# FFN stages of a two-model kernel: third block's split ahead of the norm's variance, squares inside the second block, row sums a block later

## The chip, the cores and the metric

One core of one Trainium2 chip. The metric is the device time of one execution in microseconds; three runs of the kernel before were timed, and one more execution was profiled. TensorE multiplies matrices into PSUM, ScalarE (ACT) and VectorE (DVE) do the elementwise work, GpSimd (POOL) helps with both, SyncE (SP) issues the large transfers.

## The reference

Two stacks of two layers each, over one sequence of 256 tokens of width 1024 (fp32). The first stack modulates each stage by vectors computed from a condition `c`; the second has plain RMS norms:

```python
# first stack, for l in 0, 1
mod = silu(c) @ mod_w[l] + mod_b[l]              # nine vectors of 1024: shift, scale, gate of three stages
f = swiglu(modulate(x, sh1, sc1), ffn_in[l, 0], ffn_out[l, 0])
x = deepnorm_residual(x, f, g1, ln_g[l, 0], ln_b[l, 0], 0.5)
...                                              # a mixer (even or odd), then a second FFN in the same form
# second stack, for i in 0, 1
h = x + 0.5 * swiglu_2(rms_norm_2(x, norm_ffn1[i]), w_ffn1_in[i], w_ffn1_out[i])
...                                              # window attention and a convolution
h = h + 0.5 * swiglu_2(rms_norm_2(h, norm_ffn2[i]), w_ffn2_in[i], w_ffn2_out[i])
x = h + (p[i] @ w_pe_proj[i]) * sigmoid(rms_norm_2(h, norm_pe[i]) @ w_pe_gate[i])

def swiglu_2(x, w_in, w_out):
    gate, up = split(x @ w_in, 2)
    return (silu(gate) * up) @ w_out
def rms_norm_2(x, g, eps=1e-6):
    return x * rsqrt(mean(x * x) + eps) * g
```

The inner width of an FFN is 2816.

## The kernel before

**Stream of weights.** All weights pass as a stream of 1 MB blocks (128 x 2048 fp32) through a ring of four slots `raw`. SyncE issues the transfer of block n when block n-4 is done (`blk_done`). A matmul in fp32 is made of three in a rounded format, so each block is split: ScalarE writes the high part, `whi` (`split_hi`, line 471), VectorE the rest, `wlo` (`split_lo`, line 1039), and TensorE waits for it (`split_ready`). Both splits run `AHEAD` = 2 blocks ahead of the block in hand. Each engine has its own program, and its instructions run in the order written; a helper `catch_up` makes the split of the second block of a stage inside the norm ahead of it.

**An FFN.** 22 blocks go up (a gate block and a value block form a pair, 11 pairs), 11 go down. In the first stack `ffn_pair` is the elementwise work of a pair, in the second `ffn2_pair`. The up stage runs as a loop of five turns of two pairs, and the last pair stands behind the loop.

**Second stack.** The activations go into TensorE before they are divided by the norm's root, and the factor is applied to the result. `wide_block` (lines 1879 and 1881) writes high and low parts side by side into one of two banks pairs, `ab` and `mb`. `ffn2_pair` on ScalarE copies the low half out (655), splits the next block, applies Silu (658), copies the second low half (660), splits, and rounds the product (664). On VectorE it adds the low half to the bank (1095), multiplies by `rstd` (1097, which also frees the bank), splits, adds for the second bank (1101), multiplies with GpSimd's part (1105, which frees the second bank), splits, and writes `h_lo`. GpSimd multiplies the gate by `rstd` (445).

**The norm ahead of it** (`norm2`, with `which` 0 and 2 ahead of FFNs): VectorE updates x, ScalarE writes `u_hi` and squares (632), VectorE writes `u_lo` (1323) and sums the squares (1329); TensorE sums them over partitions (`squares`, 2123) behind the first block; ScalarE takes the Sqrt (649) and VectorE the reciprocal (1362), at the end of `norm2`. The split of the third block comes behind all this, inside the first pair.

**First stack, down stage.** `d_block` (1987) does a down block. The vectors of the modulation are summed over partitions on the side: VectorE multiplies slices of `mod_w` by `c` and adds them (1127, 1130), ScalarE makes the high part of such a vector (`vec_high`, 522; for v >= 2 it waits for the sums of vector v-2), GpSimd the low part (`vec_low`, 414), TensorE sums them (`mod_rows`, 2045 and 2046; it waits for the take of the vector before), and VectorE takes the result (`mod_take`: 1143 for a gate, 1148 and 1152 for the others). The first and third FFN have six vectors, five of them in this stage, the second has three and the fourth one. With many vectors VectorE also has one product step 1130 behind each split.

## Time and profile before

| | us |
|---|---|
| median of 3 runs (2372.4 to 2381.05) | 2380.95 |
| the profiled execution | 2381.47 |
| its span, from first to last instruction | 2379.7 |
| TensorE matmuls busy | 2258.0 |
| VectorE busy | 1733.5 |
| ScalarE busy | 1232.8 |
| GpSimd busy | 219.3 |

The profile's page lists busy times, and the trace behind it each instruction. A row of a timeline has start, duration, engine, line, operation, written and read tiles, and in brackets how long the engine had been idle before it and what ended that. The mean granted clock of TensorE was 0.986 of its full level.

### The profile page before, as it was taken

What the parts mean: (1) busy time and instruction counts of PE and PEld (TensorE: products, weight loads), DVE (VectorE), ACT (ScalarE), POOL (GpSimd) and SP (SyncE); (2) the same over time, 40 slices, a digit from 0 to 9 for tenths busy, and PEclk for the clock granted to TensorE, in tenths of its full rate; (3) what the DMA queues carried; (4) which work ended last, traced back from release to release, by engine and by line L of the source; (5) the groups of instructions that cost most, each with busy time, mean ns of one, the idle gap of its engine ahead of it and who ended that gap; (6) DMA issues with size and microseconds to landing.
All of it is one profiled execution on the core that took longest, in us unless ns stands there. A gap on an engine that the chain in (4) does not pass through costs nothing.

```text
span 2379.7 us, 38110 instructions
## 1 busy us (share of the span) xinstructions
PE 2258.0 (95%) x15380; PEld 2072.6 (87%) x15380; DVE 1733.5 (73%) x1813; ACT 1232.8 (52%) x1301; POOL 219.3 (9%) x199
## 2 busy tenths in 40 slices
PE   4999889999999998999999999999999999999999
PEld 4997788799889877799788997988998899798899
DVE  5997786796589976755677569977567756996665
ACT  2443555454454545455466454666456636466644
POOL 0123000010201300000021000011001100001200
PEclk9999999999999999899999999999999999999999
DMA  8996432586568752455455542445454554345453
GB/s 345 350 357 230 153 142 108 214 312 259 194 236 355 299 209 91 160 212 179 175 190 189 186 154 104 158 179 188 183 182 159 189 182 160 107 153 179 181 188 135
DMA packets 75934, 471.49 MB, mean 198 GB/s; under 512 B 8707, under 2 KB 8963, under 8 KB 27580
## 3 DMA queue, kind: packets, MB, share of 16 engines
q1 hardware_dynamic: 53136, 383.80, 43.7%
q0 software_dynamic: 18976, 68.71, 7.7%
q10 hardware_dynamic: 3724, 17.56, 2.0%
q8 instruction: 75, 1.23, 0.2%
q14 instruction: 23, 0.19, 0.0%
HBM read 468.97 MB, written 1.06 MB: 198 GB/s over the span
## 4 chain that ended last, share of the span: by engine, by line
PE 77%; DVE 12%; ACT 6%; DMA 3%; issue 2%; ACTq 0%; SPq 0%; DVEq 0%
PE ab L1848 30%; PE acc L1848 13%; PE acc L1987 9%; PE ab L1879 7%; PE mb L1879 6%; DVE wlo L1039 3%; PE ab L1881 3%; PE mb L1881 3%; ACT whi L471 2%; DMA raw<-stream 2%; PE mb L2234 1%; DMA par<-params 1%; DVE sc L1659 1%; PE acc L2262 1%; DVE sc L1130 1%
## 5 line engine op out<-in xcount | busy, mean ns | idle before, releaser
L1039 DVE TENSOR_TENSOR wlo<-raw,whi 128x2048 fp32r<-128x2048 f32 x361 | 827.3, 2295 | 317.2 <-ACT whi L471 315.2
L471 ACT ACTIVATE whi<-raw 128x2048 fp32r<-128x2048 f32 x361 | 689.4, 1912 | 472.9 <-DMA raw<-stream 297.7
L1848 PE MATMUL ab<-uu,whi 128*128 128x256 f32 x4512 | 830.4, 287 | 25.2 <-DVE uu L1227 11.7
L1848 PEld LDWEIGHTS ab<-uu,whi 128*128 128x128 f32 x4512 | 711.6, 194 | 40.1 <-issue 22.8
L1848 PE MATMUL ab<-uu,wlo 128*128 128x256 f32 x2256 | 643.2, 285 | 0.0
L1848 PEld LDWEIGHTS ab<-uu,wlo 128*128 128x128 f32 x2256 | 437.7, 194 | 0.0
L1848 PE MATMUL acc<-h_hi,whi 128*128 128x256 f32 (+1 forms) x1032 | 293.8, 285 | 4.3 <-ACT sc L853 1.6
L1848 PE MATMUL acc<-h_hi,wlo 128*128 128x256 f32 (+1 forms) x1032 | 292.4, 283 | 0.0
L1848 PE MATMUL acc<-h_lo,whi 128*128 128x256 f32 (+1 forms) x1032 | 292.4, 283 | 0.0
L1879 PE MATMUL ab<-uu,whi 128*128 128x512 f32 x704 | 252.0, 400 | 8.7 <-DVE uu L1323 4.9
L1879 PE MATMUL mb<-uu,whi 128*128 128x512 f32 x704 | 249.9, 398 | 0.0
L1848 PEld LDWEIGHTS acc<-h_hi,whi 128*128 128x128 f32 x1032 | 197.7, 192 | 6.1 <-DVE h_lo L1743 2.0
L1881 PE MATMUL ab<-uu,wlo 128*128 128x256 f32 x704 | 198.4, 282 | 0.0
L1848 PEld LDWEIGHTS acc<-h_lo,whi 128*128 128x128 f32 x1032 | 197.7, 192 | 0.1
L1848 PEld LDWEIGHTS acc<-h_hi,wlo 128*128 128x128 f32 x1032 | 197.7, 192 | 0.0
L1881 PE MATMUL mb<-uu,wlo 128*128 128x256 f32 x704 | 197.4, 280 | 0.0
L445 POOL TENSOR_TENSOR sc<-sc,rstd 128x512 f32<-128x512 f32 x44 | 98.2, 2231 | 991.4 <-ACT sc L658 991.4
L1879 PEld LDWEIGHTS ab<-uu,whi 128*128 128x128 f32 x704 | 133.6, 190 | 42.6 <-issue 9.5
L1879 PEld LDWEIGHTS mb<-uu,whi 128*128 128x128 f32 x704 | 132.6, 188 | 31.4
L1130 DVE SCALAR_TENSOR_TENSOR sc<-modmem,cact,sc 128x1024 f32 (+1 forms) x112 | 152.3, 1360 | 8.2 <-DVE h_lo L1086 2.7
L1987 PE MATMUL acc<-whi,h_hi 128*128 128x512 f32 x448 | 148.7, 396 | 2.5 <-DVE wlo L1039 2.5
L1987 PE MATMUL acc<-wlo,h_hi 128*128 128x512 f32 x448 | 147.6, 394 | 0.0
(338 smaller groups left out, 2734.7 us busy)
## 6 DMA issues: line engine op xcount, KB each, us to landing
raw<-stream SPq DMA_DIRECT2D x365, 1024.0 KB, 4.8
modmem<-mods POOLq DMA_DIRECT2D x128, 512.0 KB, 6.1
sc<-lnrows ACTq DMA_DIRECT2D x5, 1024.0 KB, 5.2
sc<-start ACTq DMA_DIRECT2D x4, 1024.0 KB, 16.7
gateb<-gaterows ACTq DMA_DIRECT2D x6, 512.0 KB, 3.7
hank<-toep POOLq DMA_DIRECT2D x8, 192.0 KB, 3.8
x<-xT ACTq DMA_DIRECT2D x1, 1024.0 KB, 31.5
x<-xn ACTq DMA_DIRECT2D x1, 1024.0 KB, 4.8
```

What stands on the lines that cost most here:

```text
L445: nc.gpsimd.tensor_tensor(gated, gated, r, ALU.mult).then_inc(g2_ready, 1)
L471: nc.scalar.activation(whi[:, n % RAW, :], raw[:, n % RAW, :], ACT.Copy).then_inc(hi_ready, 1)
L1039: nc.vector.tensor_tensor(wlo[:, n % RAW, :], raw[:, n % RAW, :], whi[:, n % RAW, :].bitcast(F32), ALU.subtract).then_inc(lo_ready, 1)
L1130: nc.vector.scalar_tensor_tensor(out=out, in0=part, scalar=cact[:, k:k + 1], in1=out, op0=ALU.mult, op1=ALU.add).then_inc(mod_done, 1)
L1659: ins = nc.vector.scalar_tensor_tensor(out=sc[:, 28 + c, :], in0=cpad[:, c, t:t + T], scalar=w, in1=sc[:, 28 + c, :], op0=ALU.mult, op1=AL ...
L1848: ins = nc.tensor.matmul(out, l, r, start=first and i == 0, stop=last and i == 2, skip_group_check=True)
L1879: nc.tensor.matmul(bank[:, m, :].rearrange("p (a t) -> p a t", a=2), wh[:, k, m * P:m * P + P], uu[:, :, k, :], start=k == 0, stop=k == DM ...
L1881: ins = nc.tensor.matmul(bank[:, m, 0:T], wl[:, k, m * P:m * P + P], u_hi[:, k, :], start=False, stop=k == DM - 1, skip_group_check=True)
L1987: ins = nc.tensor.matmul(acc[:, 2 * t + c, :], l, w[:, k, 512 * c:512 * c + 512], start=first and k == 0 and w is wh and l is hh, stop=las ...
L2234: ins = nc.tensor.matmul(mb[:, k % 2, o:o + w], l, r, start=(c == 0), stop=(c == len(terms) - 1), skip_group_check=True)
L2262: ins = nc.tensor.matmul(out, v(h, kt), turned(k)[:, kt * T:kt * T + T], start=(kt == 0), stop=(kt == 1))
```

## The change

- `norm2` with `which` 0 or 2: ScalarE splits the third block (`split_hi(g[0] + AHEAD)`) behind the squares and ahead of the wait for the variance; VectorE makes its part behind the sums of squares. The wait for the root and the reciprocal leave `norm2` for these two norms.
- `ffn2`: the first pair is written out ahead of the loop (the last one joins the loop). It has no split in its first half, and VectorE does the reciprocal in it, behind the first add.
- `ffn2_pair`: the add frees the bank, and a separate count `sum_made` tells ScalarE of the products.
- Layer 1's first FFN of the second stack (`ffn2(late=True)`): TensorE does the squares inside the second wide block, half way.
- First stack: `mod_rows(f, v)` stands ahead of block v+3 and no longer v+2, with the take on VectorE ahead of the split of j = v+3 and no longer behind that of j = v+2; `mod_save` and `mod_cols` move from j = 7 to 8.
- `ffn` is written for the first stack alone. That changes no order.

```diff
 # ScalarE
@@ norm2
                 cnt["x"] += 4
                 cnt["var"] += 1
+                if which % 2 == 0:
+                    split_hi(g[0] + AHEAD)
                 act.wait_ge(var_ready, cnt["var"])
@@ ffn2_pair
-            def ffn2_pair(n, k, j, it):
+            def ffn2_pair(n, k, j, it, first=False):
                 b = a[0] + 2 * k
                 done(n + 2 * k, it)
                 nc.scalar.activation(spare_lo[:, 0], part_lo(b), ACT.Copy).then_inc(ylo_ready, 1)
-                split_hi(n + 2 * k + AHEAD, it)
-                act.wait_ge(bank_evac[b % 2], at(b // 2 + 1, it, 2))
+                if not first:
+                    split_hi(n + 2 * k + AHEAD, it)
+                act.wait_ge(sum_made, at(2 * cnt["made"] + 2 * k + 1, it, 4))
                 nc.scalar.activation(gated, gated, ACT.Silu).then_inc(silu_ready, 1)
                 done(n + 2 * k + 1, it)
                 nc.scalar.activation(spare_lo[:, 1], part_lo(b + 1), ACT.Copy).then_inc(ylo_ready, 1)
                 split_hi(n + 2 * k + 1 + AHEAD, it)
-                act.wait_ge(bank_evac[(b + 1) % 2], at((b + 1) // 2 + 1, it, 2))
+                act.wait_ge(sum_made, at(2 * cnt["made"] + 2 * k + 2, it, 4))
@@ ffn2
+            def ffn2(beside=None):
+                ffn2_pair(g[0], 0, 0, None, True)
...
+                with act.Fori(0, 5) as it:
+                    for j in range(2):
+                        ffn2_pair(g[0], j, j + 1, it)
...
 # VectorE
@@ ffn2_pair
-                nc.vector.tensor_tensor(gated, part_hi(b), spare_lo[:, 0], ALU.add).then_inc(sum_made, 1)
-                dve.wait_ge(sum_made, at(2 * cnt["g2"] + 2 * k + 1, it, 4))
+                nc.vector.tensor_tensor(gated, part_hi(b), spare_lo[:, 0], ALU.add).then_inc(bank_evac[b % 2], 1)
+                dve.wait_ge(bank_evac[b % 2], at(b // 2 + 1, it, 2))
+                if first:
+                    dve.wait_ge(std_ready, cnt["std"])
+                    nc.vector.reciprocal(rstd[:, 0, :], rstd[:, 0, :]).then_inc(rinv_ready, 1)
+                    dve.wait_ge(rinv_ready, rinv)
                 nc.vector.tensor_tensor(gated, gated, rstd[:, 0, :].unsqueeze(1).broadcast_to([P, 2, T]),
-                                        ALU.mult).then_inc(bank_evac[b % 2], 1)
-                split_lo(n + 2 * k + AHEAD, it)
+                                        ALU.mult).then_inc(sum_made, 1)
+                if not first:
+                    split_lo(n + 2 * k + AHEAD, it)
...
-                    .then_inc(sum_made, 1)
-                dve.wait_ge(sum_made, at(2 * cnt["g2"] + 2 * k + 2, it, 4))
+                    .then_inc(bank_evac[(b + 1) % 2], 1)
+                dve.wait_ge(bank_evac[(b + 1) % 2], at((b + 1) // 2 + 1, it, 2))
                 dve.wait_ge(g2_ready, at(cnt["g2"] + k + 1, it, 2))
-                nc.vector.tensor_tensor(prod, gated, spare_lo[:, 1], ALU.mult)\
-                    .then_inc(bank_evac[(b + 1) % 2], 1)
+                nc.vector.tensor_tensor(prod, gated, spare_lo[:, 1], ALU.mult).then_inc(sum_made, 1)
@@ ffn (first stack), down stage
                 for j in range(FFN_B - 1):
+                    if 3 <= j <= min(vecs, 5) + 2:
+                        mod_take(f, j - 3)
                     split_lo(g[0] + j + AHEAD)
                     if vecs > 5 and j < DM:
                         mod_block(f, 5 * DM + j, None, j)
-                    if 2 <= j <= min(vecs, 5) + 1:
-                        mod_take(f, j - 2)
-                    if j == 7:
+                    if j == 8:
                         mod_save(f, 1)
                         mod_cols(GATE_AT[f])
@@ norm2
                 sum_squares(3)
+                if which % 2 == 0:
+                    split_lo(g[0] + AHEAD)
                 cnt["sq"] += 4
                 cnt["std"] += 1
-                dve.wait_ge(std_ready, cnt["std"])
-                nc.vector.reciprocal(rstd[:, 0, :], rstd[:, 0, :]).then_inc(rinv_ready, 1)
-                dve.wait_ge(rinv_ready, 4 * l + which + 1)
+                if which % 2:
+                    dve.wait_ge(std_ready, cnt["std"])
+                    nc.vector.reciprocal(rstd[:, 0, :], rstd[:, 0, :]).then_inc(rinv_ready, 1)
+                    dve.wait_ge(rinv_ready, 4 * l + which + 1)
 # TensorE
@@ wide_block
+                    if between is not None and (k, m) == (0, 1):
+                        between(acc[:, 3, 0:T])
@@ ffn (first stack)
                 for i in range(FFN_B - 2):
-                    if 2 <= i <= min(vecs, 5) + 1:
-                        mod_rows(f, i - 2)
+                    if 3 <= i <= min(vecs, 5) + 2:
+                        mod_rows(f, i - 3)
@@ ffn2
-            def ffn2():
+            def ffn2(late=False):
                 wide_block(g[0], a[0], None, True)
                 cnt["u"] += 4
-                squares(acc[:, 3, 0:T])
-                wide_block(g[0] + 1, a[0] + 1)
+                if not late:
+                    squares(acc[:, 3, 0:T])
+                wide_block(g[0] + 1, a[0] + 1, None, False, squares if late else None)
```

## Rows read from the trace of the kernel before

**Rows 1.** The page, busy time: us (share of the span) xinstructions.

```profile
PE 2258.0 (95%) x15380; PEld 2072.6 (87%) x15380; DVE 1733.5 (73%) x1813; ACT 1232.8 (52%) x1301; POOL 219.3 (9%) x199
```

**Rows 2.** Timeline of TensorE, first FFN's down stage.

```profile
183.54 0.39 PE L2045 MATMUL mb<-uu,mean_r 128*128 128x512 f32 x1
...
193.81 0.47 PE L2045 MATMUL mb<-uu,mean_r 128*128 128x512 f32 x1 [3.75 <-issue]
...
201.88 0.40 PE L2045 MATMUL mb<-uu,mean_r 128*128 128x512 f32 x1
```

**Rows 3.** Timeline of VectorE, same stage.

```profile
189.19 3.38 DVE L1130 SCALAR_TENSOR_TENSOR sc<-modmem,cact,sc 128x1024 f32<-128x1024 f32 x1
192.50 1.21 DVE L1143 SCALAR_TENSOR_TENSOR gateb<-mb,gateb 128x1024 f32<-128x1024 f32 x1
```

**Rows 4.** Timeline of TensorE, third FFN's down stage.

```profile
824.42 0.77 PE L2045 MATMUL mb<-uu,mean_r 128*128 128x512 f32 x1 [5.05 <-issue]
...
833.46 0.39 PE L2045 MATMUL mb<-uu,mean_r 128*128 128x512 f32 x1
```

**Rows 5.** Timeline of TensorE, last pair of both down stages.

```profile
232.99 0.47 PE L1987 MATMUL acc<-whi,h_hi 128*128 128x512 f32 x1 [0.95 <-DVE wlo L1039]
...
864.42 0.47 PE L1987 MATMUL acc<-whi,h_hi 128*128 128x512 f32 x1 [0.81 <-DVE wlo L1039]
```

**Rows 6.** Timeline of TensorE, starts of FFNs A, B, C.

```profile
1202.20 0.49 PE L1879 MATMUL ab<-uu,whi 128*128 128x512 f32 x1 [1.13 <-DVE wlo L1039]
...
1573.36 0.49 PE L1879 MATMUL ab<-uu,whi 128*128 128x512 f32 x1 [1.04 <-DVE wlo L1039]
...
1579.01 0.39 PE L1879 MATMUL mb<-uu,whi 128*128 128x512 f32 x1
...
1789.35 2.07 PE L2123 MATMUL acc<-sc,mean_r 128*128 128x256 f32 x4 [2.24 <-DVE sc L1329]
...
1798.11 0.49 PE L1879 MATMUL ab<-uu,whi 128*128 128x512 f32 x1 [0.60 <-DVE wlo L1039]
```

**Rows 7.** Windows: stretch, length, engines' busy us, PEclk (granted clock), DMA share, GB/s.

```profile
195.00:198.40 3.40, 3.40 (x9) 2.63 (x9) 3.37 (x3) 2.86 (x2) 2.24 (x1) 0.51 0.24 95
```

**Rows 8.** Line 1130 in the whole trace: ns min/median/max, first and last start.

```profile
L1130 DVE SCALAR_TENSOR_TENSOR sc<-modmem,cact,sc x112: 1277/1285/3435, 59.9 to 1020.7; 128x1024 f32 x91, 128x1024 f32<-128x1024 f32 x21
```

**Rows 9.** Timeline of GpSimd, first FFN's down stage.

```profile
187.96 3.54 POOL L414 TENSOR_TENSOR uu<-sc,uu 128x1024 fp32r<-128x1024 f32 x1
```

**Rows 10.** DMA issues at 221 to 222 us: KB each, us to landing.

```profile
raw<-stream SPq DMA_DIRECT2D x1, 1024.0 KB, 7.2
```

**Rows 11.** Timeline of ScalarE, start of FFN A.

```profile
1195.56 0.48 ACT L649 ACTIVATE rstd<-acc,par 128x256 f32<-128x256 f32 x1 [5.88 <-PE acc L2123]
```

**Rows 12.** Timeline of ScalarE, start of FFN B.

```profile
1563.12 1.28 ACT L649 ACT_TABLE_LOAD   x1
...
1568.50 0.60 ACT L655 ACTIVATE sc<-ab 128x512 f32<-128x512 f32 x1
1568.99 1.91 ACT L471 ACTIVATE whi<-raw 128x2048 fp32r<-128x2048 f32 x1
...
1572.21 0.63 ACT L658 ACTIVATE sc<-sc 128x512 f32<-128x512 f32 x1
```

**Rows 13.** Timeline of VectorE, start of FFN B.

```profile
1567.21 1.75 DVE L1362 RECIPROCAL rstd<-rstd 128x256 f32<-128x256 f32 x1 [2.74 <-ACT rstd L649]
1569.18 0.69 DVE L1095 TENSOR_TENSOR sc<-ab,sc 128x512 f32<-128x512 f32 x1 [0.21 <-ACT sc L655]
...
1575.16 2.29 DVE L1039 TENSOR_TENSOR wlo<-raw,whi 128x2048 fp32r<-128x2048 f32 x1
```

**Rows 14.** DMA issue at 1560.3 us (FFN B), and at 2156.0 (D).

```profile
raw<-stream SPq DMA_DIRECT2D x1, 1024.0 KB, 5.5
...
raw<-stream SPq DMA_DIRECT2D x1, 1024.0 KB, 4.8
```

**Rows 15.** Timeline of ScalarE, first FFN's down stage.

```profile
195.01 1.06 ACT L522 ACTIVATE uu<-sc 128x1024 fp32r<-128x1024 f32 x1 [4.50 <-PE mb L2046]
```

More of the change, by code:

```diff
@@ L661, in ffn2_pair @@
                 split_hi(n + 2 * k + 1 + AHEAD, it)
[L662 removed]
+                act.wait_ge(sum_made, at(2 * cnt["made"] + 2 * k + 2, it, 4))
                 o = bass.ds(at(2 * j, it, 4), 2)
                 nc.scalar.activation(h_hi[:, o, :], prod, ACT.Copy).then_inc(hhi_ready, 1)
+            def ffn2(beside=None):
+                ffn2_pair(g[0], 0, 0, None, True)
+                g[0] += 2
+                a[0] += 2
+                cnt["made"] += 1
+                with act.Fori(0, 5) as it:
+                    for j in range(2):
+                        ffn2_pair(g[0], j, j + 1, it)
+                cnt["made"] += 10
+                g[0] += 20
+                a[0] += 20
+                with act.Fori(0, 2) as it:
+                    for j in range(RAW):
+                        split_hi(g[0] + j + AHEAD, it)
+                if beside is not None:
+                    beside()
+                for j in range(8, FFN_B - 1):
+                    split_hi(g[0] + j + AHEAD)
+                g[0] += FFN_B
+                ph[0] += 1
             def gate_blocks(func, n):
@@ L1178, in ffn, with ffn2 @@
                         for j in range(2):
-                            pair(g[0], j, j, it)
+                            ffn_pair(g[0], j, j, it)
+                g[0] += 20
+                a[0] += 20
+                cnt["hhi"] += 10
+                ffn_pair(g[0], 0, 10, None)
+                g[0] += 2
+                a[0] += 2
+                cnt["hhi"] += 1
+                for j in range(FFN_B - 1):
+                    if 3 <= j <= min(vecs, 5) + 2:
+                        mod_take(f, j - 3)
+                    split_lo(g[0] + j + AHEAD)
+                    if vecs > 5 and j < DM:
+                        mod_block(f, 5 * DM + j, None, j)
+                    if j == 8:
+                        mod_save(f, 1)
+                        mod_cols(GATE_AT[f])
+                g[0] += FFN_B
+                ph[0] += 1
+            def ffn2(i, beside=None):
+                ffn2_pair(g[0], 0, 0, None, True, 2 * i + 1)
+                g[0] += 2
+                a[0] += 2
+                cnt["hhi"] += 1
+                cnt["g2"] += 1
+                with dve.Fori(0, 5) as it:
+                    for j in range(2):
+                        ffn2_pair(g[0], j, j + 1, it)
                 g[0] += 20
@@ L1866, in a_block, with wide_block @@
                 ins.then_inc(blk_done, 1)
-            def wide_block(n, an, it=None, first=False):
+            def wide_block(n, an, it=None, first=False, between=None):
                 split_ready(n, it)
```

89 lines of the change are left out of this document (33 added, 56 removed).

## Prediction

> **What bounds the kernel now.** I read the page's busy shares first: TensorE is busy 95% of the span [rows 1], so a change pays only where it removes TensorE idle time, or where a longer path reaches TensorE. Next I took the timeline of TensorE in the stretches that the diff touches and looked at the bracket behind each row, the idle time before it. Five kinds of place matter. (1) Down stage of the first FFN: TensorE reaches the sums of vector 1 at 190.1 (193.81 less 3.75) and starts them at 193.81 [rows 2]. The bracket says "issue", which names nobody, so I went to VectorE: its gate product L1143 ends at 193.71 (192.50 + 1.21) [rows 3]. That is `mod_take(f, 0)`, and `mod_rows(f, 1)` waits for `modrow_taken`, so this is the true releaser. (2) The third FFN has the same stall, 5.05 us [rows 4]. (3) At the end of both down stages TensorE waits 0.95 and 0.81 us for the last split [rows 5]. (4) In each of the four FFNs of the second half the third block waits for its split: 1.13, 1.04 and 0.60 us [rows 6], and 1.04 again in the fourth of them. (5) In layer 1's first FFN the squares of the norm hold TensorE for 2.24 us [rows 6]. Call these four FFNs A, B, C, D in order of time.
>
> **Row sums a block later (first half).** Nothing is added; order alone changes. On TensorE the sums of vector v stand ahead of block v+3, not v+2. On VectorE the take of v stood behind the split of j=v+2 and now stands ahead of that of j=v+3, which is the same place. So VectorE's gate product of vector 0 still ends by 193.7, but TensorE now needs it only ahead of block 4. One stride (a block and its sums) is 190.1 - 183.54 = 6.5 us [rows 2]; 24 of its 28 matmuls are the block's, so a block alone is about 5.6. TensorE does block 3 straight from 190.1 and asks at about 195.7: slack 2.0 us. In the third FFN it would reach 824.42 - 5.05 = 819.4, run block 3 and ask at 825.0 for a product that ended just before 824.42: slack 0.6 us [rows 4]. So both stalls go. With them goes the slow stretch behind each: the granted clock is 0.51 at 195.0 to 198.4, right behind the idle time [rows 7], that is the 1.2 GHz level, and the stride from 193.81 to 201.88 is 8.1 us where 6.5 is normal; in the third FFN it is 833.46 - 824.42 = 9.0. Gain: 3.75 + 1.6 = 5.3 and 5.05 + 2.5 = 7.6.
>
> The third FFN's slack is thin, so I look at what VectorE does ahead of the product. In the first FFN its product step L1130 takes 3.38 us against 1.28 at best [rows 3, 8], while GpSimd's low half L414 runs from 187.96 [rows 9]; the third FFN's stage has the same order. GpSimd's next low half (vector 2) waits for ScalarE's high half, which stands behind split j=2 and waits for the row sums of vector 0; those come a block later, so the low half starts about when VectorE's step has begun, and no longer ahead of it. That can only shorten the path to the gate product. If nothing shortens, the slack stays 0.6; if the step were lengthened once more by 2.1 us, TensorE would wait 1.5.
> The Trainium skill (SBUF — State Buffer, section "SBUF: two separate sides") calls the pair shared by VectorE and GpSimd "an exclusive lock, not a bandwidth split": who starts first keeps it. By that rule the step would run in its short form and the slack would be near 2.7 us; the sum is the same.
>
> The last block's wait: its transfer, issued at block 6's end, lands 7.2 us later [rows 10], and the two splits follow. The last pair used to start with two blocks in between; now the sums of vector 4 stand in that interval too, some 0.9 us more, so 0.95 and about 0.8 of the waits [rows 5] are covered: 1.7. Together the first half gives 5.3 + 7.6 + 1.7 = 14.6. The second and fourth FFN have no such idle time (3 vectors and 1): 0. The save and column steps on VectorE move one split later and still end ahead of the norm that reads them: 0, covered by blocks 9 and 10.
>
> **Third block split ahead of the variance (second half).** ScalarE now splits block 3 before its Sqrt and VectorE follows before the first pair; the reciprocal moves behind the first add. What the third block waited for is then there early. But look what is late next: the fourth block. Its split on ScalarE stands behind the first Silu, and that now waits for this chain, counted from the Sqrt's start: Sqrt 0.5, copy of the low half 0.60, add 0.69, reciprocal 1.75, product 0.69 as the add, Silu 0.63, second copy 0.60, split 1.91, rest of the split on VectorE 2.29 [rows 12, 13]: 9.7 us. Before, the reciprocal ran beside a table load and a copy on ScalarE, and cost the chain nothing. VectorE's rest of the third split now stands ahead of the add; it ends about when the copy does (2.29 us behind the split's end, against Sqrt and copy behind the load), so it adds nothing. A block is 5.65 us (1573.36 to 1579.01) [rows 6]. So the fourth block starts at the later of "third block's start + 5.65" and "Sqrt's start + 9.7".
> A: Sqrt at 1195.56 [rows 11] gives 1205.3; the third block starts at 1201.1, the fourth is due at 1206.7. Gain 1.1.
> B: the transfer of the third block is issued at 1560.3 and lands 5.5 us later [rows 14]; the split takes 1.91, and a table load of 1.28 that used to stand hidden at 1563.12 [rows 12] now stands behind it. Sqrt at 1569.1, fourth block at 1578.8, due at 1578.0. Gain 1.04 - 0.85 = 0.2.
> D: the same, with a landing of 4.8 us [rows 14]: gain 1.0.
> C: the transfer is there. The squares stand inside the second block, half of it (2.8 us) behind 1787.1, at 1789.9 to 1790.2, and the Sqrt follows some 1.2 us later (the four take 2.07 us at half clock [rows 6], so 1.0, and a handover), at 1791.2. Fourth block at 1800.9; before it started at 1798.11 + 5.65 = 1803.8. Gain 2.9, where the idle times and the half clock behind them promise 4.2.
> Sum 5.2. Bounds: if the table load stays ahead of the split, 6.1; if both transfers take 7.2 us, 1.0. I take 5.2, since both landings have rows of their own place.
> The Trainium skill (ScalarE: Activation LUTs, section "What ACT_TABLE_LOAD costs") adds a drain of some 1.38 us to each switch, 2.66 in all. Here the Silu at 1572.21 starts right behind its load, so the trace shows no such drain [rows 12]; by the page B and D would lose 2.8 more.
>
> **Bank free with the sum.** TensorE gets a wide bank back one VectorE step earlier. No TensorE row in these stages waits for an add or a product, so it is worth 0; its cover is the other bank's block of 5.65 us. Its new price is a separate count for the product, the same waits as before.
>
> **Sum.** 14.6 + 5.2 = 19.8 us. The profiled execution took 2381.47 us (span 2379.7), beside a median of 2380.95: 2381.5 - 19.8 = 2361.7; against the median 2361.2. I give 2361.5.
>
> **Rivals.** (a) The first-half stalls stay: TensorE asks a block later but meets another late party, the low half or the split of block 5. For it: the bracket says "issue", so the releaser is my inference, and the slack in the third FFN is thin. Against: the gate product ends within 0.1 us of TensorE's start. It leaves 5.2 us: 2376.3. (b) The fourth block is not late (load ahead, short landings, short chain): 7.3 in the second half, 2381.5 - 21.9 = 2359.6. (c) A switch of tables holds ScalarE for twice its row, 1.28 us more [rows 12]; in B and D that lies on the chain, 2.6 in all: 2364.3. For it speaks the page on tables named above, against it the row of the Silu. (d) Slower: ScalarE's high half of vector v (v = 2, 3, 4) waits for the sums of v-2 (4.50 us already) [rows 15], and those come a block later; behind it on ScalarE stands the split of the next weight block, and for that split waits VectorE, then TensorE. It has 1.06 + 1.91 + 2.29 = 5.3 us of work against two blocks and a sum, 12 us. It decides once more than 6.7 us comes on top (a late transfer and long VectorE steps together). Then each of the 7 such vectors costs up to a block, 5.6 us: 39 us, less 5.2 from the second half: 2415. The change doing nothing at all would need (a) and four late fourth blocks.
>
> **How the numbers follow.** Forecast 0.70 (its own range 2356 to 2367), (a) 0.12, (b) 0.09, (c) 0.05, (d) 0.04. The range: downwards (b) and the run of 2372.4 among the three before, which shows that one execution can lie 8.6 us lower, so 2354; upwards (c), the lower bound of the second half (4.2 more) and a part of (a), 2372. A difference of 0.5%, 11.9 us, is about what a measurement here tells from no change; the line is 2369. Faster takes the forecast, (b) and (c) less a little for one that lands half way to (a): 0.81. Same: 0.15. Slower: (d), 0.04.
>
> **What would show it.** In the first and third FFN's down stage no TensorE idle time over 0.3 us ahead of L2045, the granted clock at its full level there, and the gate product ending ahead of TensorE's sums. At the end no wait ahead of the last pair. In the second half a third block without a bracket in A to D; in B and C a new bracket ahead of the fourth block's first matmul, near 0.9 and 1.5 us; a table load between ScalarE's split and the Sqrt in B and D. It is wrong if L2045 still has a bracket, if splits of blocks 5 to 8 in the down stage hold TensorE, or if the half clock appears at new places.

## The result and the profile after

The changed kernel takes 2358.17 us (median of six runs, 2352.44 to 2363.68), the kernel before 2378.6 us in as many: ratio 0.992, 95% interval 0.9907 to 0.9932, so 20.4 us faster. The forecast was 2361.5 with a range of 2354 to 2372. The profiled execution took 2359.93 us, its span is 2357.7 us against 2379.7. The head of its page (busy us, share of the span, instructions):

```profile
span 2357.7 us, 38158 instructions
...
PE 2250.4 (95%) x15380; PEld 2066.6 (88%) x15380; DVE 1732.9 (73%) x1813; ACT 1185.2 (50%) x1265; POOL 238.4 (10%) x199
```

TensorE is busy 7.6 us less than in [rows 1] with the same matmuls, and idle 14.4 us less (107.3 for 121.7). The first number is the clock: fewer matmuls ran at its lower level (stretches at a granted clock of one half add up to 51.7 us for 70.2). Of these 18.5 us fewer, 10.2 stood at the two stalls of the first half and 3.4 under the squares of C; the other 4.9 lie elsewhere. ScalarE's 47 us less are 36 table loads of 1.28 us: before, the second half's FFN pair had 20 loads at its first copy and 20 at its Silu, one of each in every turn of the four loops; now that the first pair stands ahead of the loop, 4 are left. Behind the fourth block TensorE's wide blocks have no bracket in either kernel, so of all these loads only those around the first pair can matter, and they stand in the chains below.

**First FFN's down stage**, timeline of TensorE, VectorE and GpSimd (start, duration, engine, line, operation, out<-in; in brackets the idle time ahead of it and what ended it). The row sums are now L2082, the product step L1152 (L1130 before), the gate product L1165 (L1143), the split L1057 (L1039):

```profile
188.55 1.27 DVE L1152 SCALAR_TENSOR_TENSOR sc<-modmem,cact,sc 128x1024 f32<-128x1024 f32 x1
188.69 0.39 PE L2082 MATMUL mb<-uu,mean_r 128*128 128x512 f32 x1
...
189.81 1.23 DVE L1165 SCALAR_TENSOR_TENSOR gateb<-mb,gateb 128x1024 f32<-128x1024 f32 x1
...
190.96 2.41 POOL L414 TENSOR_TENSOR uu<-sc,uu 128x1024 fp32r<-128x1024 f32 x1 [3.67 <-ACT uu L522]
...
195.06 0.39 PE L2082 MATMUL mb<-uu,mean_r 128*128 128x512 f32 x1
```

The 3.75 us of [rows 2] are gone: the sums of vector 1 start at 195.06 without a bracket, 6.37 us behind those of vector 0. The gate product ends at 191.04, 4.0 us ahead of them. The product step takes 1.27 us for the 3.38 of [rows 3]: GpSimd's low half starts at 190.96, when the step has ended (189.82). The clock, by windows (busy us and count of each engine, granted clock, DMA share, GB/s), where [rows 7] had 0.51, and in the third FFN's down stage:

```profile
195.00:198.40 3.40, 3.40 (x16) 2.79 (x16) 3.37 (x4) 2.22 (x2) 1.06 (x1) 1.00 0.83 294
198.40:237.00 38.60, 38.60 (x173) 31.78 (x172) 33.28 (x33) 16.14 (x12) 6.39 (x7) 1.00 0.61 217
...
826.00:856.00 30.00, 30.00 (x134) 24.78 (x133) 25.74 (x25) 12.35 (x8) 4.53 (x5) 1.00 0.69 243
```

TensorE is busy for the whole of the second and third window, which hold the last pairs: their waits [rows 5] are gone too. **Third FFN's down stage**, the same engines:

```profile
812.10 2.39 POOL L414 TENSOR_TENSOR uu<-sc,uu 128x1024 fp32r<-128x1024 f32 x1 [1.20 <-ACT uu L522]
...
812.16 3.43 DVE L1152 SCALAR_TENSOR_TENSOR sc<-modmem,cact,sc 128x1024 f32<-128x1024 f32 x1
...
815.51 1.21 DVE L1165 SCALAR_TENSOR_TENSOR gateb<-mb,gateb 128x1024 f32<-128x1024 f32 x1
...
816.82 0.47 PE L2082 MATMUL mb<-uu,mean_r 128*128 128x512 f32 x1 [0.47 <-issue]
```

Here 0.47 us of the 5.05 [rows 4] are left. GpSimd's low half started 0.06 us ahead of the product step, the step took its long form, and the gate product ended at 816.72. That is one execution: in the second profile of the changed kernel and in the six others that follow with the sums at this place, the step started first in both stages and took 1.27 us, and no bracket stands at the sums.

**Second half, FFN B**, ScalarE and TensorE (Sqrt L644, Silu L654; L1119 is VectorE's product):

```profile
1547.73 1.92 ACT L471 ACTIVATE whi<-raw 128x2048 fp32r<-128x2048 f32 x1 [2.60 <-DMA raw<-stream]
1549.66 1.28 ACT L644 ACT_TABLE_LOAD   x1
1550.95 0.47 ACT L644 ACTIVATE rstd<-acc,par 128x256 f32<-128x256 f32 x1
...
1555.19 0.63 ACT L654 ACTIVATE sc<-sc 128x512 f32<-128x512 f32 x1 [1.97 <-DVE sc L1119]
...
1556.21 1.91 ACT L471 ACTIVATE whi<-raw 128x2048 fp32r<-128x2048 f32 x1
...
1560.49 0.50 PE L1916 MATMUL mb<-uu,whi 128*128 128x512 f32 x1 [0.46 <-DVE wlo L1057]
```

The third block has no bracket in A, B, C or D. The table load stands between the third split and the Sqrt, as the prediction said, and the fourth block waits 0.46 us for its split: it starts 9.54 us behind the Sqrt's start. The chain holds a second table load, 1.28 us at 1551.94 ahead of the Silu; it costs nothing, since ScalarE still waits 1.97 us behind it for the product. In C the same chain is 9.53 us (Sqrt, then the fourth block):

```profile
1774.87 0.47 ACT L644 ACTIVATE rstd<-acc,par 128x256 f32<-128x256 f32 x1 [3.48 <-PE acc L2161]
...
1784.40 0.50 PE L1916 MATMUL mb<-uu,whi 128*128 128x512 f32 x1 [1.11 <-DVE wlo L1057]
```

One measure compares the second half over all kernels: the time from the first matmul of the first wide block to that of the fifth, in us, read off TensorE's timeline. A star marks a stretch at half clock inside.

| kernel | A | B | C | D |
|---|---|---|---|---|
| before | 27.63* | 24.56 | 29.86* | 24.76 |
| row sums only | 27.63* | 24.79 | 28.91 | 24.76 |
| changed | 26.24* | 24.20 | 26.78 | 23.64 |
| row sums where they were | 26.24* | 23.67 | 26.91* | 23.62 |
| squares not late | 26.24* | 24.18 | 27.61* | 23.59 |
| bank freed by the product | 27.84* | 24.92 | 27.30 | 23.93 |
| split ahead of Silu | 26.55* | 23.48 | 25.39* | 23.47 |
| split ahead of Silu, again | 26.55* | 23.71 | 25.55 | 23.47 |
| reciprocal back | 26.56* | 23.64 | 27.96* | 23.48 |
| row sums two blocks later | 26.24* | 23.87 | 26.87 | 23.52 |
| two blocks later, take back | 26.55* | 25.58 | 26.82* | 23.57 |
| two blocks later, split ahead | 26.55* | 23.20 | 25.34* | 23.48 |
| changed again | 26.24* | 25.69 | 26.78* | 23.57 |

Not every star costs time. In A it lies in the first block, and the second starts 9.4 us behind it all the same; only in "bank freed by the product" did it fall on the squares and the second block, and there A is 1.6 us longer.

The change saves 1.39, 0.36, 3.08 and 1.12 us here, 5.95 together; against the kernel with the row sums alone, whose squares of C ran at full clock, 1.39 + 0.59 + 2.13 + 1.12 = 5.2. In B the kernels with the changed order differ among themselves by 2 us; why, stands under "Landing times" at the end.

### The profile page after: what moved, and what is told of

Same layout as the page of the kernel before. It is cut to its first block, busy times and chain, and to the rows that moved or that the text cites. A ratio compares the mean times of both kernels' runs of the same rounds, so it can differ in the third digit from the quotient of the medians.

```text
span 2357.7 us, 38158 instructions
## 1 busy us (share of the span) xinstructions
PE 2250.4 (95%) x15380; PEld 2066.6 (88%) x15380; DVE 1732.9 (73%) x1813; ACT 1185.2 (50%) x1265; POOL 238.4 (10%) x199
## 4 chain that ended last, share of the span: by engine, by line
PE 76%; DVE 12%; ACT 5%; DMA 4%; issue 2%; ACTq 0%; DVEq 0%; SPq 0%
PE ab L1883 27%; PE acc L1883 13%; PE acc L2024 10%; PE mb L1916 7%; PE ab L1916 6%; DVE wlo L1057 4%; PE mb L1918 3%; PE ab L1918 3%; ACT whi L471 2%; DMA raw<-stream 2%; PE mb L2272 1%; DMA modmem<-mods 1%; DMA par<-params 1%; DVE sc L1694 1%; PE acc L2300 1%
## 5 line engine op out<-in xcount | busy, mean ns | idle before, releaser
L1057 DVE TENSOR_TENSOR wlo<-raw,whi 128x2048 fp32r<-128x2048 f32 x361 | 829.0, 2300 | 299.3 <-ACT whi L471 296.4
L445 POOL TENSOR_TENSOR sc<-sc,rstd 128x512 f32<-128x512 f32 x44 | 119.9, 2726 | 964.2 <-ACT sc L654 964.2
L1152 DVE SCALAR_TENSOR_TENSOR sc<-modmem,cact,sc 128x1024 f32 (+1 forms) x112 | 150.2, 1341 | 9.5 <-DMA modmem<-mods 3.7
L426 POOL DMA_DIRECT2D modmem<-mods x128 | 68.5, 536 | 795.0 <-DVE sc L1149 570.6
```

What stands on the lines that cost most here:

```text
L426: pool.dma_start(modmem[:, i % MODRING, :], mods[i]).then_inc(mod_in[i % MODRING], 16)
L445: nc.gpsimd.tensor_tensor(gated, gated, r, ALU.mult).then_inc(g2_ready, 1)
L1057: nc.vector.tensor_tensor(wlo[:, n % RAW, :], raw[:, n % RAW, :], whi[:, n % RAW, :].bitcast(F32), ALU.subtract).then_inc(lo_ready, 1)
L1152: nc.vector.scalar_tensor_tensor(out=out, in0=part, scalar=cact[:, k:k + 1], in1=out, op0=ALU.mult, op1=ALU.add).then_inc(mod_done, 1)
```

## Experiments

### The two halves apart

Row sums a block later, put into the kernel before, and nothing else:

```diff
 # TensorE, ffn
-                    if 2 <= i <= min(vecs, 5) + 1:
-                        mod_rows(f, i - 2)
+                    if 3 <= i <= min(vecs, 5) + 2:
+                        mod_rows(f, i - 3)
```

(with VectorE's take and save as in the change).

> The kernel before with the row sums a block later and nothing else. Theory (TensorE waited for VectorE's gate product alone, and the half clock came from that wait): 14.6 us less than before, a ratio near 0.994; no bracket over 0.5 us ahead of the row sums, the second half's brackets as before (1.13, 1.04, 2.24 and 0.60, 1.04). Rival (the party that is late is another one, GpSimd's low half or a split): under 5 us less, and a bracket of 2 us or more at the row sums.

Measured: 2363.9 us beside 2378.63 for the kernel before, ratio 0.9941 (0.9925 to 0.9956): 14.7 us. No bracket over 0.3 us at the row sums or the last pair of either down stage, full clock over both. By windows, the first:

```profile
186.00:206.00 20.00, 20.00 (x89) 16.50 (x88) 18.99 (x12) 8.61 (x6) 9.02 (x7) 1.00 0.77 263
```

The counterpart, the changed kernel with the row sums back where they were (the same edit the other way):

> The changed kernel with the row sums where they were. Theory: 5.2 us less than before, ratio near 0.998; the brackets of 3.75 and 5.05 us ahead of the row sums are back, the fourth blocks of B and C wait 0.5 and 1.1 us as in the changed kernel. If the two parts helped each other through the clock, the two gains of this run and of the one with the row sums alone would not add up to the whole (20.4 us).

Measured: 2374.21 us, ratio 0.9983 (0.9971 to 0.9996), 4.4 us under the kernel before. The stalls return, with VectorE's gate product ending just ahead of each (timeline of both engines, then windows):

```profile
190.02 3.38 DVE L1152 SCALAR_TENSOR_TENSOR sc<-modmem,cact,sc 128x1024 f32<-128x1024 f32 x1
193.33 1.21 DVE L1165 SCALAR_TENSOR_TENSOR gateb<-mb,gateb 128x1024 f32<-128x1024 f32 x1
...
194.64 0.77 PE L2082 MATMUL mb<-uu,mean_r 128*128 128x512 f32 x1 [4.75 <-issue]
...
824.27 0.77 PE L2082 MATMUL mb<-uu,mean_r 128*128 128x512 f32 x1 [4.99 <-issue]
```

```profile
193.90:200.70 6.80, 6.06 (x14) 4.79 (x15) 6.70 (x6) 2.86 (x2) 3.20 (x3) 0.50 0.30 114
822.00:828.80 6.80, 4.53 (x11) 3.60 (x12) 6.76 (x5) 2.80 (x3) 1.87 (x2) 0.50 0.57 204
```

What follows: 14.7 and 4.4 us add up to 19.1 of 20.4, and the missing 1.3 us are well inside the intervals (10.5 to 17.8 us for the first, 1 to 7 for the second). C's fourth block waits 1.09 us, as expected; B's does not wait, where 0.5 was expected. The releaser that the profile calls "issue" is the take of the vector before: in this kernel it ends at 194.54, TensorE starts at 194.64. The lower clock, 0.50, belongs to the stall in these two stages: it comes with it and goes with it.

### Squares behind the first block again

```diff
-                ffn2(l == 1)
+                ffn2()
```

> The changed kernel with layer 1's first squares behind the first block again. Theory (the fourth block of C starts 9.5 us behind the Sqrt's start, whatever the place of the squares): TensorE waits some 2.2 us ahead of the squares again, the wait ahead of the fourth block (1.11 us) falls below 0.3, and the fourth block starts within 0.5 us of where it does in the changed kernel, counted from the first block's start; up to 1.7 us more if the half clock comes back. Rival (the place of the squares is worth its idle time): 2.2 us or more later at the fourth block, with its bracket still there.

Measured: 2358.21 us, ratio 0.992 (0.9902 to 0.9938). In C the squares wait on TensorE, and the fourth block doesn't (timeline of TensorE):

```profile
1770.22 1.13 PE L2161 MATMUL acc<-sc,mean_r 128*128 128x256 f32 x4 [1.90 <-DVE sc L1361]
...
1782.50 0.40 PE L1916 MATMUL mb<-uu,whi 128*128 128x512 f32 x1
```

So the late squares take away a wait of 1.90 us and give back 1.11: 0.8 us, as in the table (27.61 for 26.78). Counted from the first block the fourth starts 0.84 us later than in the changed kernel, where my theory allowed 0.5: the place of the squares is worth a little in itself, far less than the rival's 2.2 us. The half clock lay in its first block, which still took 7.8 us (7.64 in the changed kernel), because it covered waits for `u_lo` there. C's other 1.3 us (28.91 to 27.61) come from the third split.

### The bank freed by the product

```diff
 # VectorE, ffn2_pair
-                nc.vector.tensor_tensor(gated, part_hi(b), spare_lo[:, 0], ALU.add).then_inc(bank_evac[b % 2], 1)
+                nc.vector.tensor_tensor(gated, part_hi(b), spare_lo[:, 0], ALU.add).then_inc(sum_made, 1)
...
-                                        ALU.mult).then_inc(sum_made, 1)
+                                        ALU.mult).then_inc(bank_evac[b % 2], 1)
...
```

(the second bank in the same form, and ScalarE's two waits with them).

> The changed kernel with the bank freed by the product again. Theory (the reciprocal now stands between add and product, so the product is late for the third block): the third block waits for the product in B (some 0.8 us), C (1.4) and D (0.4), not in A; the fourth starts 0.4 us later in each of the three, 1.3 us in all. Rival, the record's own line (bank free with the sum is worth 0): no bracket ahead of a third block.

Measured: 2359.59 us, ratio 0.9931 (0.9906 to 0.9956). The third block now waits for the bank in B, C and D (timeline of TensorE):

```profile
1552.49 0.50 PE L1916 MATMUL ab<-uu,whi 128*128 128x512 f32 x1 [1.16 <-DVE sc L1119]
...
1776.82 0.50 PE L1916 MATMUL ab<-uu,whi 128*128 128x512 f32 x1 [1.51 <-DVE sc L1119]
...
2148.49 0.49 PE L1916 MATMUL ab<-uu,whi 128*128 128x512 f32 x1 [0.40 <-DVE sc L1119]
```

These 3.07 us take the place of the fourth block's waits (0.46 and 1.11), so by the table the early bank is worth 0.7 us in B, 0.5 in C and 0.3 in D: 1.5 us. Of B's 0.7, up to 0.36 can be a later landing: ScalarE's third split starts 6.04 us behind the first block there and 5.68 in the changed kernel. That leaves 1.2 to 1.5 us. The times don't resolve that; the rows do.

### The chain ahead of the fourth block, cut in two ways

First, in the first pair alone, the fourth block's split ahead of the Silu on ScalarE, and on VectorE behind the product with the reciprocal:

```diff
 # ScalarE, ffn2_pair
-                if not first:
-                    split_hi(n + 2 * k + AHEAD, it)
+                split_hi(n + 2 * k + AHEAD + first, it)
...
-                split_hi(n + 2 * k + 1 + AHEAD, it)
+                if not first:
+                    split_hi(n + 2 * k + 1 + AHEAD, it)
```

(VectorE's `split_lo` in the same form).

> The changed kernel with one thing moved: in the first pair of each second-half FFN the fourth block's split stands ahead of the Silu on ScalarE, and on VectorE right behind the product with the root's reciprocal. Nothing is added. My theory: the fourth block is late in B and C because its split stands behind the chain Sqrt, sum, reciprocal, product, Silu, second copy (9.5 us). Ahead of the Silu it is out of that chain: ScalarE then splits about 0.6 us behind the Sqrt, so that the fourth block's brackets of 0.46 (B) and 1.11 us (C) go, 1.6 us in all, and TensorE has no new idle time over 0.3 us at the fifth or sixth block, although the Silu comes 1.9 us later (the second pair's first bank is needed only by block 5). Span about 2356 at the same share of half clock. Rival: the transfer of the fourth block, or the last part of the third block's split, sets the fourth block's start: then B's bracket stays near 0.46. Second rival: the later Silu and product move the wait to the fifth block, with a bracket of 0.3 to 1.5 us there.

Measured: 2358.36 us, ratio 0.9936 (0.992 to 0.9952). In C the split runs while VectorE does the reciprocal, and the fourth block starts 8.1 us behind the Sqrt, straight behind the third (timelines of ScalarE, VectorE, TensorE):

```profile
1769.89 0.48 ACT L644 ACTIVATE rstd<-acc,par 128x256 f32<-128x256 f32 x1 [3.54 <-PE acc L2161]
...
1770.74 1.92 ACT L471 ACTIVATE whi<-raw 128x2048 fp32r<-128x2048 f32 x1
1772.68 1.28 ACT L653 ACT_TABLE_LOAD   x1
1774.12 0.63 ACT L653 ACTIVATE sc<-sc 128x512 f32<-128x512 f32 x1 [0.16 <-DVE sc L1119]
...
1774.01 2.28 DVE L1057 TENSOR_TENSOR wlo<-raw,whi 128x2048 fp32r<-128x2048 f32 x1
...
1778.02 0.39 PE L1916 MATMUL mb<-uu,whi 128*128 128x512 f32 x1
```

Both brackets are gone, none has come at the fifth block. C is the evidence, since its third transfer had long landed in all kernels. In B the landing was early (the third split starts 5.12 us behind the first block, 5.68 in the changed kernel), and with such a landing the changed order has no bracket either (5.16 us, in the kernel with the row sums where they were). The Silu starts 4.2 us behind the Sqrt, as before: the split fills time in which ScalarE had waited 1.97 us for the product. Neither rival of this run holds.

Second, the reciprocal back at the norm's end, ahead of the sum:

```diff
 # VectorE, norm2
-                if which % 2:
-                    dve.wait_ge(std_ready, cnt["std"])
-                    nc.vector.reciprocal(rstd[:, 0, :], rstd[:, 0, :]).then_inc(rinv_ready, 1)
+                dve.wait_ge(std_ready, cnt["std"])
+                nc.vector.reciprocal(rstd[:, 0, :], rstd[:, 0, :]).then_inc(rinv_ready, 1)
```

> The changed kernel with the reciprocal back at the end of the norm, ahead of the first pair's sum on VectorE. My theory: then the reciprocal (1.75 us) runs beside ScalarE's copy of the low half (0.58) and the sum waits for the reciprocal and no longer the other way round, so the chain from the Sqrt to the fourth block's split is some 0.6 us shorter, 8.9 for 9.5 us. In B the bracket of 0.46 ahead of the fourth block goes, in C it falls from 1.11 to about 0.5. The price: the sum, which frees the bank, comes 1.1 us later, so the third block waits for the bank in C for about 0.8 us and in B for about 0.4. Rival: the order doesn't matter, the chain stays 9.5 us and the brackets stay. Times within 1 us of the changed kernel's by both.

Measured: 2360.78 us, ratio 0.9928 (0.9911 to 0.9945). In C (timelines of ScalarE, VectorE and TensorE; the wide block is L1911 here):

```profile
1777.21 0.47 ACT L644 ACTIVATE rstd<-acc,par 128x256 f32<-128x256 f32 x1 [5.08 <-PE acc L2156]
...
1777.71 1.75 DVE L1392 RECIPROCAL rstd<-rstd 128x256 f32<-128x256 f32 x1 [1.83 <-ACT rstd L644]
1779.50 0.69 DVE L1113 TENSOR_TENSOR sc<-ab,sc 128x512 f32<-128x512 f32 x1
...
1780.24 0.51 PE L1911 MATMUL ab<-uu,whi 128*128 128x512 f32 x1 [0.25 <-DVE sc L1113]
...
1786.26 0.50 PE L1911 MATMUL mb<-uu,whi 128*128 128x512 f32 x1
```

The chain is 9.05 us for 9.53, near the 8.9 expected, and the fourth block's bracket is gone in C (the block starts 6.0 us behind the third, where a block without any wait takes 5.7). B has none either, but its landing was early again (5.20 us), so B shows nothing of this edit. The price was over-estimated: the third block waits 0.25 us for the bank, where 0.8 stood, and not at all in B. Counted from the Sqrt, TensorE reached the third block at 2.78 us, and VectorE had read the bank at 2.98 (at 1.68 in the changed kernel): the sum does come 1.3 us later, but nearly all of that falls into time in which TensorE was still busy with the second block.

### Row sums two blocks later

```diff
 # TensorE, ffn                                   (VectorE: take at j >= 4, save at j = 9)
-                    if 3 <= i <= min(vecs, 5) + 2:
-                        mod_rows(f, i - 3)
+                    if 4 <= i <= min(vecs, 5) + 3:
+                        mod_rows(f, i - 4)
```

> The changed kernel with the row sums (and the take, the save and the column step) one more block later: sums of vector v ahead of block v+4. My theory: a further block of slack takes the last 0.47 us ahead of the sums of vector 1 in the third FFN's down stage away and changes nothing else: 0.5 us, not to be told from no change by the times, with full clock in both stages. Rival (the slower case of the prediction): ScalarE's high half of vector v, v = 2 to 4, waits for the sums of v-2, and the split of the next block stands behind it; with the sums yet a block later this wait grows by 5.6 us a vector, and blocks 5 to 8 of the down stage wait for VectorE's split, 1 to 5 us each, 10 us and more in all. If this shows brackets, the slack that the prediction gave (6.7 us beyond the change) was too large.

Measured: 2382.57 us, ratio 1.003 (1.0017 to 1.0043): 24 us above the changed kernel and slower than the one before. My theory fell. Timelines of TensorE, ScalarE and VectorE in the first FFN's down stage, from the last matmul of one vector's sums to the first of the next:

```profile
194.82 0.39 PE L2083 MATMUL mb<-uu,mean_r 128*128 128x512 f32 x1
...
195.24 1.06 ACT L522 ACTIVATE uu<-sc 128x1024 fp32r<-128x1024 f32 x1 [10.34 <-PE mb L2083]
196.21 1.90 ACT L471 ACTIVATE whi<-raw 128x2048 fp32r<-128x2048 f32 x1
...
198.14 2.79 DVE L1057 TENSOR_TENSOR wlo<-raw,whi 128x2048 fp32r<-128x2048 f32 x1 [6.93 <-ACT whi L471]
200.86 1.27 DVE L1152 SCALAR_TENSOR_TENSOR sc<-modmem,cact,sc 128x1024 f32<-128x1024 f32 x1
202.06 1.21 DVE L1165 SCALAR_TENSOR_TENSOR gateb<-mb,gateb 128x1024 f32<-128x1024 f32 x1
...
203.37 0.63 PE L2082 MATMUL mb<-uu,mean_r 128*128 128x512 f32 x1 [2.72 <-issue]
```

It is a ring. The sums of vector v release ScalarE's high half of v+2, the split of the next block stands behind that, VectorE's split behind it, then the product step, and only then the take of vector v; the sums of v+1 wait for that take. Round it goes in 8.2 us (195.21 to 203.37), where a block is 5.6. The stage has brackets of 2.72, 1.87 and 1.69 us at the sums and 1.22 at the last pair, 7.5 in all, and two stretches of 3.4 us at half clock, worth another 3.4; from its start to its end it takes 76.3 us for 64.6. The third FFN shows the same (2.72, 1.83, 1.68, 1.21; 76.3 for 65.6). Together 22.4 us of the 24. The second FFN, with three vectors, has one bracket of 1.52 us at the sums and 0.57 at the last pair, and takes 65.3 us for 63.1.

The ring can be opened without moving the sums: VectorE's take one split earlier.

```diff
-                    if 4 <= j <= min(vecs, 5) + 3:
-                        mod_take(f, j - 4)
+                    if 3 <= j <= min(vecs, 5) + 2:
+                        mod_take(f, j - 3)
```

> The kernel with the row sums two blocks later (23 us slower than the changed kernel), with VectorE's take, save point aside, back one split earlier: the take of vector v ahead of the split of j = v+3, as in the changed kernel, the sums on TensorE still ahead of block v+4. My theory of the 23 us: the sums of v+1 wait for a ring: sums of v, ScalarE's high half of vector v+2 (1.06), split (1.90), VectorE's split (2.8), its product step (1.27) and only then the take (1.21), 8.2 us against a block of 5.6. With the take ahead of that split the ring opens: the waits of 2.72, 1.87 and 1.69 us ahead of the sums of each of the two stages go. What is left is the split itself, whose chain of 5.8 us behind the sums stands against a block of 5.6: brackets of up to 0.3 us at the blocks, and perhaps the last pair's 1.2. So 2361 to 2365. Rival: the splits or the low half hold the sums, not the take; then the brackets of 1.7 to 2.7 stay, and the time stays near 2382.

Measured: 2366.23 us, ratio 0.9955 (0.9936 to 0.9973). Timelines of VectorE and TensorE:

```profile
195.48 1.22 DVE L1165 SCALAR_TENSOR_TENSOR gateb<-mb,gateb 128x1024 f32<-128x1024 f32 x1 [4.80 <-PE mb L2083]
...
200.73 0.39 PE L2082 MATMUL mb<-uu,mean_r 128*128 128x512 f32 x1
...
229.32 0.47 PE L2024 MATMUL acc<-whi,h_hi 128*128 128x512 f32 x1 [2.95 <-DVE wlo L1057]
```

All six brackets at the sums are gone, which settles the ring. The time is 1 us above the expected 2361 to 2365: the last pair waits 2.95 us in both stages, more than the 1.2 I had allowed: the take of vector 4 now comes at 220.97, ahead of the last splits (it came at 215.31 in the changed kernel), and its two steps and those behind it push them back. So the changed kernel's place for the sums is the best of the three tried.

### Looking for a better version

The split ahead of the Silu and the row sums two blocks later in one kernel:

> The changed kernel with both: the fourth block's split ahead of the Silu, and the row sums one more block later. If neither has a hidden price the two add up: 1.6 and 0.5 us, 2.1 us below the changed kernel at the same share of half clock, ratio to the kernel before 0.991 for 0.992. Rival: one of them opens a new wait (fifth block, or blocks 5 to 8 of the down stage), and the time is the changed kernel's or above it.

Measured: 2379.54 us, ratio 1.0012 (0.9998 to 1.0026). The ring is back (2.72, 2.25 and 2.73 us at the sums), and nothing else could be read from the time. The split ahead of the Silu was then run a second time, beside the changed kernel:

> The kernel with the fourth block's split ahead of the Silu, a second time and in five rounds, beside the changed kernel on the same chip. The traces of both say that from the first to the fifth wide block it saves 0.7 us in the second of the four FFNs and 1.4 in the third, and loses 0.3 in the first: 1.9 in all. If that reaches the end, its median lies 2 us under the changed kernel's; if the stretches of half clock fall anywhere in each execution, the two medians can't be told apart, since single executions of one kernel lie 11 us apart.

> The changed kernel itself, a second time and in five rounds, for a comparison on one chip: 2358, ratio to the kernel before 0.992. Its brackets ahead of the fourth block in the second and third FFN of the second half (0.46 and 1.11 us) should return within 0.1, and the half clock should be absent from both down stages of the first half; elsewhere its places may differ from those of the first profile.

Measured: 2356.18 us, ratio 0.9911 (0.9888 to 0.9935), and 2358.16 us, ratio 0.9915 (0.9893 to 0.9936). Over all their runs the medians are 2357.3 (ten runs) and 2358.2 (twelve): by the times the two can't be told apart. By the traces of this pair the version with the split ahead is 3.0 us shorter from first to fifth wide block over the four FFNs, but 2.0 of that are B, and there the third block's transfer landed 1.7 us later in the changed kernel, whose fourth block waited 1.88 us. What the edit is worth is C's 1.2 to 1.4 us; the 0.3 that A loses are the slower pace described at the end. B in the changed kernel (timelines of ScalarE and TensorE):

```profile
1548.47 1.92 ACT L471 ACTIVATE whi<-raw 128x2048 fp32r<-128x2048 f32 x1 [3.83 <-DMA raw<-stream]
...
1561.24 0.50 PE L1916 MATMUL mb<-uu,whi 128*128 128x512 f32 x1 [1.88 <-DVE wlo L1057]
```

In both profiles with the split ahead no block of B waited, but their third splits started 5.12 and 5.45 us behind the first block, for 7.16 here. That the version is also safer against a late landing is likely, as its fourth split no longer stands behind the Silu, but no run shows it.

## Why the prediction was right, and where it was not

**The releaser of the first-half stalls was named right.** The step from "issue" to VectorE's take rested on 0.1 us between two rows [rows 2, 3]. Changing that order alone gave 14.7 us for the 14.6 of the sum; that they agree to 0.1 is luck, with an interval of 10.5 to 17.8 us. By stage, from the first down block to the transposes behind the last: first FFN 71.4 to 64.6, 6.8 us (5.3 and 0.95 predicted), third FFN 73.6 to 65.6, 8.0 us (7.6 and 0.8). The half clock as part of the price was right in kind and size. Rival (a) is out.

**The third FFN's slack went both ways.** The prediction had 0.6 us if nothing shortens and said that the low half would start behind VectorE's step, "that can only shorten the path". In the profile of the change it started 0.06 us ahead of it, the step kept its 3.43 us, and TensorE waits 0.47 us. In the seven other profiles with the sums at this place the step started first, and the gate product ended 1.8 to 3.0 us ahead of TensorE's sums. The two are released by different events, the step by the end of VectorE's split and the low half by ScalarE's high half, so the order can change from one execution to the next; the bound of 1.5 us for the bad case held.
The Trainium skill (SBUF — State Buffer, section "SBUF: two separate sides") says that the pair is held by whoever starts first and that the other fully blocks. The third FFN's stage agrees in both orders. Where GpSimd started first, 812.10 + 2.39 plus a full step of 1.27 would end at 815.76, and the step ended at 815.59. In the second profile of the changed kernel VectorE started first, and the low half took the longer time, 3.21 us for 2.39:

```profile
814.51 1.27 DVE L1152 SCALAR_TENSOR_TENSOR sc<-modmem,cact,sc 128x1024 f32<-128x1024 f32 x1
814.83 3.21 POOL L414 TENSOR_TENSOR uu<-sc,uu 128x1024 fp32r<-128x1024 f32 x1 [1.58 <-ACT uu L522]
```

**Second half: the right terms, each a little small.** 5.2 us predicted; 5.95 measured against the profile before, or 4.4 by the times of the kernel without the row sums. A 1.39 for 1.1, D 1.12 for 1.0, B 0.36 for 0.2, C 3.08 for 2.9. The chain from Sqrt to fourth block came out at 9.53 us for 9.7, and its brackets at 0.46 and 1.11 for 0.9 and 1.5. B is the uncertain one: in the second execution of the changed kernel it lost 1.1 us to the kernel before, because its Sqrt now stands behind the landing of a transfer. C's 2.9 contained some 1.0 us of half clock under the squares; the row-sums kernel had the same squares at full clock (28.91 for 29.86), so that part is chance and no gain of the edit. At like clock the measured sum is 5.2, and the predicted one would have been 4.2: that 5.2 stands on both sides is luck.

**"Bank free with the sum: 0" was wrong.** It is worth 1.2 to 1.5 us, against brackets of 1.16, 1.51 and 0.40 without it. The failing step is the sentence that no TensorE row in these stages waits for a sum or product, and that the other bank's block covers it. That was read off the trace of before, where the reciprocal ran ahead of the first pair. The same change moves the reciprocal (1.75 us) between the sum and the product; with the bank freed by the product, the third block would have been late for a new reason. The prediction's total already counted no wait there, so its number did not suffer.

**Rival (b)** held for A and D, whose fourth blocks weren't late, and not for C; in B it holds or not by the landing. **Rival (c)** is out: the load at 1549.66 took 1.28 us and the Sqrt started at 1550.95. The Trainium skill (ScalarE: Activation LUTs, section "What ACT_TABLE_LOAD costs") adds a drain of about 1380 ns to each switch; here 0.01 us lay between split and load and 0.01 us between load and Sqrt, so no such time shows on either side. What the prediction said of the Silu is so too, though its load is not among [rows 12]; it ended at 1572.20, and the Silu started at 1572.21 (timeline of ScalarE before):

```profile
1570.92 1.28 ACT L658 ACT_TABLE_LOAD   x1
```

**Rival (d)** did not occur in the change, and its price was wrong in two ways. Its threshold, 6.7 us beyond the change, was that of the split reaching TensorE; the sums one block later still (5.6 us) were under it and cost 24 us, since the take stands behind that same split and closes a ring of 8.2 us first. And the price of a hit is not a block per vector, but 1.7 to 2.7 us at each of three vectors a stage, and the half clock behind.

## What to carry to other kernels

When an "issue" bracket names nobody, list what the instruction waits for in the code and look which of these ended last; then undo that order alone. Before moving a step once more in the direction that helped, follow the waits from it round to itself: the sum of that ring against one block's time says how far it may go. Judge "who waits for this" in the order of work after the change, not in the trace of before: the bank looked free until the reciprocal had moved. And where a step is moved behind work that waits for a transfer, as the Sqrt here behind the third split, plan with the scatter of the landing and not with one row of it.

## What the chip showed that was not expected

**Clock behind a stall.** Brackets of 4.75 and 4.99 us at the sums were each accompanied by 6.8 us at a granted clock of 0.50, the 1.2 GHz level. Of three brackets in one stage, 2.72, 1.87 and 1.69 us, two were followed by 3.4 us each. The waits of 1.11 and 1.88 us in C and B had none, and neither had those of 2.95 us ahead of the last pairs with the take back. So the length of a bracket alone doesn't tell whether the clock falls.

**Half clock elsewhere moves about.** A stretch of 6.8 us stood at 669.5 in the profile of before and at 660.5 to 664.6 in four others, but not in that of the changed kernel, whose code there is the same; it was back in the second profile of the changed kernel. This is 3.4 us from one execution to the next, of the kind that hides a gain of 1 to 2 us in the times. What decides it stays open.

**A wide block has two paces.** Starts of successive wide blocks lie 5.54 or 5.65 us apart, constant for a stretch and different between executions and FFNs of one kernel (A: 5.55 in the changed kernel, 5.65 with the split ahead or the reciprocal back). It is 0.1 us a block; its cause wasn't looked for. A difference of 0.1 to 0.3 us between two kernels in the table can be this alone.

**Landing times.** The third block's transfer of B ended ScalarE's wait after 2.60 us in one execution of the changed kernel and after 3.83 in the other. In the kernel before and in the one with the row sums alone the Sqrt starts 6.72 us behind B's first block in both, ahead of the third split. With the changed order it stands behind that split and starts at 8.4 to 10.4 us. All kernels with the changed order from the third split to the fourth block, in us:

| kernel | third split behind the first block | wait of the fourth block |
|---|---|---|
| row sums where they were | 5.16 | none |
| row sums two blocks later | 5.46 | 0.17 |
| changed | 5.68 | 0.46 |
| squares not late | 5.77 | 0.44 |
| two blocks later, take back | 7.05 | 1.84 |
| changed again | 7.16 | 1.88 |

So the change bought its gain in B with a dependence on the landing: up to 0.9 us better than before (24.56 to 23.67) with an early one, 1.1 worse with a late one.
